# Two mixers' loops over heads: where the halves of the gate units stand on TensorE

## The reference, cut to what matters

```python
# mixer a (layers 0 and 1)
proj = h @ w_in
ya = chunked_relpos_attention(...)      # 8 heads of 64
yb = multiscale_pool(...)
yc = forgetting_attention(...)          # 8 heads of 64
gates = sigmoid(g_lin.reshape(B, S, 3, D_MODEL))
merged = sum(gates * einsum('bsnw,nwd->bsnd', ys, w_branch))
out = merged @ w_out
# mixer b (layers 2 and 3)
u = h @ w_in
y_conv = (cb * causal_dwconv(cc * ch)) @ w_conv_out
y_attn = dilated_window_attention_in_3_groups_of_8_heads(...) @ w_attn_out
out = (sigmoid(g_conv) * y_conv + sigmoid(g_attn) * y_attn) @ w_o
```

## Time and profile before

| | |
|---|---|
| median of 3 runs | 2690.7 us (2689.76 to 2691.24) |
| profiled execution, its own time | 2691.13 us |
| its span on the core | 2689.3 us, 34148 instructions |
| PE (TensorE matmul) busy | 2645.9 us, 98% |
| PEld (TensorE weight load) busy | 2215.4 us, 82% |
| DVE (VectorE) busy | 1985.9 us, 74% |
| ACT (ScalarE) busy | 1297.3 us, 48% |
| POOL (GpSimd) busy | 0.8 us |
| DMA | 634.21 MB, mean 236 GB/s |
| mean granted TensorE clock | 0.997 |

### The profile page before, as it was taken

How to read it: one execution, slowest core, us unless ns; L and a number is a source line. 1 busy time by engine, 2 the same in 40 slices (tenths; PEclk the granted TensorE clock), 3 DMA queues, 4 the chain that set the end, 5 groups by cost and what they waited for, 6 DMA issues and landing times.

```text
span 2689.3 us, 34148 instructions
## 1 busy us (share of the span) xinstructions
PE 2645.9 (98%) x13939; PEld 2215.4 (82%) x13939; DVE 1985.9 (74%) x2251; ACT 1297.3 (48%) x1451; POOL 0.8 (0%) x6
## 2 busy tenths in 40 slices
PE   7999999999999999999999999999999999999998
PEld 4888877888888887888888899878888889997887
DVE  5777888877767888867867767677777686767744
ACT  3444565544444556544544534554454454446543
POOL 0000000000000000000000000000000000000000
PEclk8999999999999999999999999999999999999999
DMA  7886864677686874677677768547768768663752
GB/s 281 296 292 215 305 211 174 233 260 257 241 287 242 292 244 161 205 272 257 236 263 255 253 207 266 183 147 273 256 218 277 260 225 268 232 231 117 251 199 90
DMA packets 324643, 634.21 MB, mean 236 GB/s; under 512 B 12418, under 2 KB 92482, under 8 KB 324488
## 3 DMA queue, kind: packets, MB, share of 16 engines
q1 hardware_dynamic: 311952, 620.78, 67.4%
q10 hardware_dynamic: 12536, 11.25, 1.5%
HBM read 630.88 MB, written 8.97 MB: 238 GB/s over the span
## 4 chain that ended last, share of the span: by engine, by line
PE 90%; DVE 7%; issue 1%; ACT 1%; DMA 1%; ACTq 0%; DVEq 0%
PE bank L1519 19%; PE bank L1521 19%; PE bank L1520 19%; PE acc L1519 8%; PE acc L1521 8%; PE acc L1520 8%; DVE w_both L1005 2%; PE bank L1643 1%; PE bank L1580 1%; PE bank L1814 1%; DVE softmax L1220 1%; DMA raw<-in_ffn_up_all 1%; ACT w_both L577 0%; DVE x L1068 0%; DVE temp L1219 0%
## 5 line engine op out<-in xcount | busy, mean ns | idle before, releaser
L1005 DVE TENSOR_TENSOR w_both<-raw,w_both 128x2048 fp32r<-128x2048 f32 x412 | 941.7, 2289 | 489.2 <-ACT w_both L577 488.4
L577 ACT ACTIVATE w_both<-raw 128x2048 fp32r<-128x2048 f32 x412 | 786.9, 1912 | 541.6 <-PE bank L1521 326.2
L1519 PE MATMUL bank<-w_both,h 128*128 128x512 f32 (+1 forms) x2016 | 774.1, 384 | 6.4 <-DVE w_both L1005 2.9
L1521 PE MATMUL bank<-w_both,h 128*128 128x512 f32 (+1 forms) x2016 | 759.3, 377 | 0.0
L1520 PE MATMUL bank<-w_both,h 128*128 128x512 f32 (+1 forms) x2016 | 758.4, 376 | 0.0
L1519 PEld LDWEIGHTS bank<-w_both,h 128*128 128x128 f32 x2016 | 380.1, 189 | 81.5 <-DVE w_both L1005 7.4
L1521 PEld LDWEIGHTS bank<-w_both,h 128*128 128x128 f32 x2016 | 379.8, 188 | 70.9
L1520 PEld LDWEIGHTS bank<-w_both,h 128*128 128x128 f32 x2016 | 380.5, 189 | 66.3 <-issue 1.0
L1039 DVE SCALAR_TENSOR_TENSOR ada_sum<-raw,c_act,ada_sum 128x512 f32<-128x512 f32 x476 | 357.5, 751 | 14.1
L1519 PE MATMUL acc<-w_both,y 128*128 128x512 f32 x896 | 356.4, 398 | 0.0
L1521 PE MATMUL acc<-w_both,y 128*128 128x512 f32 x896 | 349.5, 390 | 0.0
(11 more groups left out here) (215 smaller groups left out, 2350.3 us busy)
## 6 DMA issues: line engine op xcount, KB each, us to landing
raw<-in_w_ada_all SPq DMA_DIRECT2D x136, 1024.0 KB, 5.2
raw<-in_w_in SPq DMA_DIRECT2D x128, 1024.0 KB, 5.7
raw<-in_ffn_gate_all SPq DMA_DIRECT2D x88, 1024.0 KB, 5.1
raw<-in_ffn_up_all SPq DMA_DIRECT2D x88, 1024.0 KB, 5.3
raw<-in_ffn_down_all SPq DMA_DIRECT2D x88, 1024.0 KB, 5.0
raw<-in_w_branch SPq DMA_DIRECT2D x12, 1024.0 KB, 7.2
first_w<-in_w_ada_all SPq DMA_DIRECT2D x8, 1024.0 KB, 14.6
raw<-in_w_out SPq DMA_DIRECT2D x8, 1024.0 KB, 5.0
```

The source lines that it names most:

```text
L577: activate(halves_of[n][0], src, ACT.Copy).then_inc(high_ready.sem, 1)
L1005: tensor(halves_of[n][1], raw_of("unit", s, k, 0)[0], halves_of[n][0].bitcast(F32), ALU.subtract).then_inc(low_ready.sem, 1)
L1519: mm(dst, a_h, b_h, start=start, stop=False, skip_group_check=True)
L1521: return mm(dst, a_l, b_h, start=False, stop=True, skip_group_check=True)
```

## The change

In both loops over heads TensorE does both halves (`tt` 0 and 1) of a gate unit in the even step, one behind the other, and none in the odd step. The orders of VectorE, ScalarE and the queues stay as they are, and so do all waits and counts.

```diff
@@ -1830,8 +1830,9 @@
                             turn(i - 1)
                         if kind == "b" and i == count:
                             between(i + 1)
-                        if i < count:
-                            gate_unit(i // 4, i // 2 % 2, i % 2)
+                        if i < count and i % 2 == 0:
+                            for tt in range(TT):
+                                gate_unit(i // 4, i // 2 % 2, tt)
                         if kind == "a":
                             between(i)
                         if i >= ago and (i - ago) % 2 == 0:
```

## The result

The changed kernel takes **2745.55 us** (median, 2744.38 to 2746.45), the kernel before 2690.23 beside it: ratio 1.0207, 95% interval 1.0194 to 1.0219, 55.3 us slower. The forecast was 2738.7, that is 48 more, in a range of 2725 to 2751. The direction, the mechanism and most of the size are as forecast; 7 us are not.

A forecast was written before the change was run, and what follows sets the result against it. TensorE's queue was taken to bound the kernel, busy 2645.9 of 2689.3 us. Mixer a's 31.3 and mixer b's 16.8 sum to 48 us on the profiled 2691.13, 2739.2, or 2738.7 against the median 2690.7; range 2725 to 2751.

The forecast's parts named there:

- Mixer a, 15.6 a loop: Predicted loss in each mixer a loop from chain, bank waits and first step; 31.3 us for two.
- the bank waits: Mixer a, steps 4, 8, 12: second half waits for ScalarE's PSUM copy, 1.30, 1.05 and 0.35 us, 2.7 in all.
- the first step: Mixer a's start: ada moves behind the whole unit, so turn(0) comes 1.7 us later.
- the chain: Mixer a, odd turn through logits to normalize and even turn: 2.95 us uncovered, seven periods 11.2 us longer.
- Mixer b, 8.4 a loop: Predicted loss in each mixer b loop, mainly 2.72 us added at steps 2, 4 and 6; 16.8 us for two.
- the end: Mixer b, step 7: from scores to the w_attn_out rows 4.27 us instead of 5.14, giving back 0.8.
- rival 3: TensorE's clock falls to 1.2 GHz in the four loops: 134 us more, 2870 us; chance 0.03.
- busy time nearly unchanged, its idle time up by some 48 us: Predicted sign for TensorE's busy and idle time in the profile after the change.
- bank waits hidden (1): Rival: waits for ScalarE's PSUM copy cost nothing, chains as forecast; 2731.5 us, chance 0.10.
- VectorE as the bound at no loss (2): Rival: VectorE sets mixer a's pace and is kept fed; 2690.7 us or up to 3 below, chance 0.03.
- further waits behind the moved halves (4): Rival: other extra waits, such as late copies of turned blocks at odd steps, 22 x 0.5; 2750 to 2755 us, chance 0.08.
- periods of 9.8 to 10.1: Predicted sign in mixer a: seven periods of this many us, later by up to 1.3 at steps 4 and 8.

The follow-up runs named there:

- e8: The change in mixer a alone, against the kernel before, with matmuls that nothing reads put into TensorE's waits there: 2723.03 us.
- e3: The changed kernel with ScalarE's copy of the second half's PSUM bank issued ahead of the step's exponentials: 2742.32 us.
- e5: The changed kernel with mixer a's first gate unit kept in halves over steps 0 and 1: 2741.22 us.
- e4: The changed kernel with VectorE's normalize ahead of logits at odd steps from 3 on in mixer a: 2733.02 us.
- e2: The change in mixer b alone, mixer a as in the kernel before: 2711.11 us.
- e9: The kernel before with whole gate units in the odd steps of mixer a, none in its even steps: 2739.83 us.
- e6: The changed kernel with the reorderings of e3 and e4, e5's split first unit, and normalize ahead of low at odd steps in mixer b: 2716.40 us.
- e12: e9 with nine unread matmuls behind the scores of even steps 2 to 14 of mixer a: 2726.40 us.

## Why the prediction was right, and where it was short

**Mixer a, 15.6 a loop: measured 16.3 at full clock** (e8, both layers). Its terms: the bank waits 2.7, measured 1.29 + 0.99 + 0.44 = 2.72 in the timeline, 2.9 by e3; the first step 1.7, measured 1.8 by e5; the chain 11.2, which leaves 16.3 - 2.9 - 1.8 = 11.6. The handover that the bare chain lacked was 0.06 a period (3.01 against 2.95), 0.4 in seven. That reading the chain from the odd turn through logits to normalize was right is shown by e4, where another order of VectorE alone takes 6.5 of it back.

**Mixer b, 8.4 a loop: measured 8.6** (e5, layer 2). The way from scores to turn (7.01), the end (4.28) and the bank wait of 0.89 (1779.83 - 1776.09 - 2.85, with the gate's start at 1776.09) stood as worked out. Of mixer b in this form only e5's layer 2 ran at full clock throughout; layer 3 is taken as equal.

**What was short.** At full clock the four loops cost 2 x 16.3 + 2 x 8.6 = 49.8, against the 48.0 of the sum. They took 56.3. The other 6.5 are the clock, for which the forecast had no term: 1.6 in each mixer a, 1.3 in layer 2 and 2.0 in layer 3. In mixer a e8 shows it, as it takes the idle time away and the fall with it. In mixer b nothing was filled; there it rests on the same code in four executions (the change, e2, e4, e5), whose eight loops grow by 8.6 without a loss, 9.8 and 9.9 with 1.7, 10.4 to 10.6 with 5.1 or 5.2 and 13.5 with 6.8. The weak step is rival 3: it priced a fall of the clock as all units at 1.2 GHz, 134 us, and so gave it 0.03 as an all-or-nothing case. The profile shows single stretches instead, which cost up to 1.7 us each and come back to 2.4 GHz in between; the loss of this execution is six of them. The argument against it, that the clock stayed at 1.00 at the waits of up to 1.57 in mixer b before, held for the waits of that kernel, not for the longer and more frequent ones that the forecast itself was adding. That the result lies inside the range is in part luck: the 12 us above the sum were meant for handovers and late copies, yet all that the sum lacked at full clock was 1.8; the clock used the room instead. The sign "busy time nearly unchanged, its idle time up by some 48 us" is off for the same reason: busy time rose by 11.7 and idle time by 43.2, since slow matmuls count as busy.

The other rivals: bank waits hidden (1) is excluded by the timeline and e3, VectorE as the bound at no loss (2) by the 49.8 us themselves and by e4, where VectorE does the same work in less time, and further waits behind the moved halves (4) did not appear, though the result lies near its band; what brought the time there was the clock. Nor did longer unbroken runs of matmuls gain anything, as one reading in the prediction would have it: a whole unit takes 5.57 us, and the loops are longer. I had named periods of 9.8 to 10.1, later at steps 4 and 8, as the sign; without clock loss (e8) they are 9.9 to 11.35, the long ones with the bank waits of 1.29, 0.99 and 0.44.

## What to carry to other kernels

A piece of TensorE work that fills the time of a chain on another engine is worth, at that place, what it covers of the chain: here all of the half unit's 2.72 us in steps 2, 4 and 6 of mixer b, and 1.7 of it a period in mixer a (11.6 in seven). Grouped with its like one step earlier it covers nothing there, and the new length is read from the timeline as the bare chain between the two instructions. Add up new waits per step and then ask what they do to the clock: here the new waits cost 49.8 us by themselves and 6.5 more through the clock, and one order (e9) lost 19.8 that way in its profiled execution. If an order must leave a wait, look first at the order of the engine that it waits for: normalize ahead of logits gave back 12.5 us without touching TensorE.

## What the runs showed of the hardware

- The granted clock fell in loops where TensorE waited 1 to 2.6 us every few microseconds, but not in each of them: e5's mixer a waits alike in both layers (up to 1.13 us) and loses 0 in one and 1.7 in the other. Waits of up to 0.67 us went with no fall (e6, mixer a). Ahead of 375:380 in the changed kernel TensorE was at work 4.48 of 5 us and then waited 1.73. The Trainium skill (TensorE: Matmul & The Clock Gate, section "HAM oscillation — how this bites in real kernels") explains such falls by long waits for a transfer between bursts; the traces here show another case, since no wait of TensorE in these loops is longer than 2.6 us and each is put down to VectorE or ScalarE, none to a transfer.
- Where the stretches fall varies between executions of nearly the same code: layer 2 lost 0, 1.7, 5.2 and 8.6 us in e5, the change, e2 and e3. In comparisons of 2 to 5 us between kernels that wait this hides the effect; the growth of a loop at clock 1.00 is the steadier measure (mixer a with whole units: 16.3 and 16.3; with filled odd units: 17.9 and 17.8). Even the kernel before has one execution, beside e12, of 2696.8 us at a mean clock of 0.995; where it fell is not known, as it was not profiled.
- Matmuls in a wait are no speed-up in themselves: e8 and e12 are slower than the kernel before by 32 and 35 us. They only gave back part of what idling had cost: 1.8 and 19.8 us in the loops of the profiled executions (34.4 to 32.6 and 55.5 to 35.7), 4.0 and 13.4 in the medians.
